# Moving ScalarE's log/exp table request and one small DVE copy in a two-layer trunk step

## The reference, cut to what matters

```python
sh1, sc1, g1, sh2, sc2, g2 = split(silu(c) @ ada_w[l] + ada_b[l], 6)
h = rms_norm(x, norm1_g[l]) * (1.0 + sc1) + sh1
x = x + g1 * mixer(h)
h = rms_norm(x, norm2_g[l]) * (1.0 + sc2) + sh2
x = x + g2 * ((silu(h @ w1) * (h @ w3)) @ w2)        # d_ff = 2816
# after both layers: y = rms_norm(x, final_norm_g)
```

## Time and profile before

| | |
|---|---|
| median of 3 runs (lowest, highest) | 1216.4 us (1214.42, 1217.55) |
| the profiled execution: time, span | 1215.29 us, 1213.5 us |
| PE busy | 1115.3 us, 92% |
| ACT busy, DVE busy, POOL busy | 399.1, 432.7, 544.4 us |
| PE's share of the chain that ended last | 72% |
| mean granted TensorE clock | 0.951 of full speed |

### The profile page before, as it was taken

How to read it: one execution, slowest core, us unless ns; L and a number is a source line. 1 busy time by engine, 2 the same in 40 slices (tenths; PEclk the granted TensorE clock), 3 DMA queues, 4 the chain that set the end, 5 groups by cost and what they waited for, 6 DMA issues and landing times.

```text
span 1213.5 us, 17339 instructions
## 1 busy us (share of the span) xinstructions
PE 1115.3 (92%) x7181; PEld 1028.0 (85%) x7181; DVE 432.7 (36%) x860; ACT 399.1 (33%) x617; POOL 544.4 (45%) x422
## 2 busy tenths in 40 slices
PE   5699998999798999999999799879998999999997
PEld 3598997896697999999999698655597999999997
DVE  4616899217665111111111230537565111111121
ACT  0532421244325322232222232447515333323221
POOL 0355576360053555455455533221053556565662
PEclk9799998899798999999999899879998999999998
DMA  9633422639525766664566821142025544434441
GB/s 311 192 105 105 140 70 70 199 132 313 157 71 139 219 196 175 184 195 142 174 211 189 219 82 42 31 101 70 2 70 139 140 110 133 129 104 129 125 123 52
DMA packets 243017, 166.46 MB, mean 137 GB/s; under 512 B 20269, under 2 KB 241532, under 8 KB 242812
## 3 DMA queue, kind: packets, MB, share of 16 engines
q1 hardware_dynamic: 214880, 135.74, 38.8%
q10 hardware_dynamic: 28060, 29.63, 7.6%
HBM read 162.43 MB, written 2.92 MB: 136 GB/s over the span
## 4 chain that ended last, share of the span: by engine, by line
PE 72%; DVE 13%; DMA 5%; POOL 4%; ACT 3%; issue 2%; ACTq 0%; SPq 0%; DVEq 0%
PE banks L431 19%; PE banks L432 18%; PE banks L433 18%; POOL w_lo L1040 4%; PE banks L505 3%; DMA raw<-in_ada_w 3%; DVE ht L1513 2%; PE banks L471 2%; ACT w_hi L1064 2%; PE banks L472 2%; PE banks L473 1%; DVE h_lo L1504 1%; DVE Kd L1697 1%; DVE Qd L1697 1%; PE banks L518 1%
## 5 line engine op out<-in xcount | busy, mean ns | idle before, releaser
L1040 POOL TENSOR_TENSOR w_lo<-raw,w_hi 128x512 fp32r<-128x512 f32 (+2 forms) x410 | 537.7, 1342 | 637.3 <-ACT w_hi L1064 637.3
L431 PE MATMUL banks<-h_hi,w_hi 128*128 128x384 f32 x1088 | 373.3, 343 | 20.8 <-DVE h_lo L1504 11.5
L432 PE MATMUL banks<-h_lo,w_hi 128*128 128x384 f32 x1088 | 368.4, 339 | 0.0
L433 PE MATMUL banks<-h_hi,w_lo 128*128 128x384 f32 x1088 | 368.1, 338 | 0.0
L1064 ACT ACTIVATE w_hi<-raw 128x2048 fp32r<-128x2048 f32 (+4 forms) x115 | 193.5, 1683 | 259.8 <-PE banks L433 169.2
L431 PEld LDWEIGHTS banks<-h_hi,w_hi 128*128 128x128 f32 x1088 | 207.3, 191 | 32.8 <-issue 29.2
L432 PEld LDWEIGHTS banks<-h_lo,w_hi 128*128 128x128 f32 x1088 | 207.3, 191 | 0.6
L433 PEld LDWEIGHTS banks<-h_hi,w_lo 128*128 128x128 f32 x1088 | 207.1, 190 | 0.6
L1567 DVE TENSOR_TENSOR uf<-sa,banks 128x384 f32<-128x384 f32 x44 | 24.4, 554 | 330.2 <-PE banks L433 324.2
L431 PE MATMUL banks<-u_hi,w_hi 128*128 128x384 f32 x352 | 119.8, 340 | 1.0 <-POOL w_lo L1040 1.0
L433 PE MATMUL banks<-u_hi,w_lo 128*128 128x384 f32 x352 | 118.3, 336 | 0.0
(11 more groups left out here) (308 smaller groups left out, 1175.8 us busy)
## 6 DMA issues: line engine op xcount, KB each, us to landing
raw<-in_ffn_w SPq DMA_DIRECT2D x88, 512.0 KB, 5.2
raw<-in_ada_w SPq DMA_DIRECT2D x28, 1024.0 KB, 7.1
raw<-in_ffn_w SPq DMA_DIRECT2D x32, 704.0 KB, 4.6
vada_raw<-in_ada_w ACTq DMA_DIRECT2D x20, 1024.0 KB, 6.6
raw<-in_w_in_even SPq DMA_DIRECT2D x18, 1024.0 KB, 5.3
raw<-in_w_out_even SPq DMA_DIRECT2D x4, 1024.0 KB, 5.9
raw<-in_w_in_odd SPq DMA_DIRECT2D x3, 1024.0 KB, 7.0
raw<-in_w_in_odd SPq DMA_DIRECT2D x8, 256.0 KB, 4.2
```

Source lines behind the costliest of these rows:

```text
L431: pe.matmul(out, s_hi, m_hi, start=first and j == 0, stop=False)
L432: pe.matmul(out, s_hi, m_lo, start=False, stop=False)
L433: mm = pe.matmul(out, s_lo, m_hi, start=False, stop=last and j == len(terms) - 1)
L1040: ins = pool.tensor_tensor(w_lo[s % SPLIT][:, at:to], raw[u % RAW][:, at:to], w_hi[s % SPLIT][:, at:to].bitcast(F32), ALU.subtract)
```

## The change

The request for the log/exp set leaves `norm` and stands once ahead of norm 0; a new request stands in `ffn` behind the loop over the 22 blocks, and the one ahead of the final norm goes. In DVE's `norm` the modulation step is done at tile 1, behind `low(0)`, where it was at tile 0 ahead of `low(0)`. Each of these places has one pair, so `modulation(place)` is the same work.

```diff
@@ ACT: def norm(n, base)
-                act.preload_act_table_set("natural_log_exp_and_others")
                 bk = misc.filled(act, ("stat", n))
@@ ACT: def ffn(l, n), loop over f
                     act.activation(u_hi[:, f, :], uf[:, f % 2, :], ACT.Copy).then_inc(S["uhi_ready"], 1)
+                act.preload_act_table_set("natural_log_exp_and_others")
                 if l == 1:
@@ DVE: def norm(n, base, place), loop over m
                     if m:
                         low(m - 1)
-                    if place is not None:
-                        modulation(place, ada_pairs(place)[m:m + 1])
+                    if place is not None and m == 1:
+                        modulation(place)
```

## The result

The changed kernel takes 1219.28 us (median of 6 runs, 1216.45 to 1221.42) where the kernel before took 1214.91 in the 6 runs beside it (1208.49 to 1217.55): a ratio of 1.0044, 95% interval 1.0024 to 1.0064. By the medians it is slower by 4.4 us; the interval goes from 2.9 to 7.8 us. The profiled execution took 1219.62 us, with a span of 1217.8.

What follows compares the result with a forecast made beforehand. PE, busy 92% of the span, was taken as the bound. Terms -0.41 - 1.44 - 0.41 + 1.35 + 1.37 = +0.46, plus 1.7 for one clock fall, gave +2.2 on 1216.4: 1218.6 us, range 1213.7 to 1220.8.

Steps and rivals of the forecast that it cites:

- The request in the FFN: Load behind each FFN's last u_hi delays the second down unit's split: 1.35 and 1.37 us slower, all on the path.
- The clock: Half clock behind PE's two lengthened down-projection waits: 45% each, one fall booked at +1.7 us, bounds 0 and 3.4.
- The row that the odds leaned on: PE's wait of 1.74 us at 792.74, followed by 3.4 us at half clock, 1.7 us of work lost.
- Two falls: Rival: clock falls at the second unit of both down projections, 1.7 us each; +3.9 in all, 1220.3 us; chance 0.16.
- The load in norms 1 and 3: Without its load Ln starts 0.79 us earlier; with the row moved, 0.41 us gained at each of norms 1 and 3.
- Norm 2: One ht and one low part go ahead of DVE's wait for PE's ada product: 1.44 us gained, bounds 0.8 and 2.2.
- Norm 0 and the final norm: Norm 0 keeps the same load at the same place; the final norm's was followed by idle ACT: 0 for both.
- A request is never skipped: Reading of the profile: the norms' request gives four real loads of 1283 ns, even where the set is loaded already.
- A drain at each load: Rival: a drain of about 1.38 us beside each new FFN load adds 2.8 us; +3.2, 1219.6 us; chance 0.02.
- hidden FFN loads: Rival: something else holds POOL's or ACT's start behind the FFN loads, only gains stay: -2.3, 1214.1 us; chance 0.06.
- the full gains of the heads: Rival: PE, not DVE's last low part, paces the first products; norms 1 to 3 give 5.4: -2.7, 1213.7 us; chance 0.06.
- the change is void: Rival: compiler puts its own load ahead of the norms' Ln, only the move gains: near 1217 us; chance 0.02.

Runs made afterwards that it cites:

- e2: Changed kernel with the FFN request one instruction earlier, directly behind the last Silu and ahead of the last u_hi: 1210.97 us, ratio 0.9982 to the kernel before.
- e5: Kernel before with only the two FFN requests added behind the last u_hi: 1220.04 us, ratio 1.0045.
- e1: The changed kernel again, unaltered: 1216.82 us, ratio 1.0027 to the kernel before.
- e3: Changed kernel with the DVE edit undone, so only the table requests change: 1216.29 us, ratio 1.0018 to the kernel before.
- e6: Changed kernel with each FFN request written twice for the same set: 1218.92 us, ratio 1.0037 to the kernel before.
- e4: Changed kernel with all ACT edits undone, so only the ada row moves: 1213.55 us, ratio 0.9995 to the kernel before.
- e7: The e2 kernel with 0.8 us of unread ACT copies added behind the last u_hi: 1212.86 us, ratio 0.9995 to the kernel before.
- e8: The e2 kernel with the ada row copied behind the norm's last low part: 1210.84 us, ratio 0.9973 to the kernel before.
- e10: The e2 kernel with the ada row back ahead of the low part of tile 0: 1212.50 us, ratio 0.9987 to the kernel before.
- e11: Same kernel as e8, timed on the chip of e10: 1210.03 us, ratio 0.9961 to the kernel before.
- e9: Changed kernel with a request for another set (exp_and_others) ahead of each FFN request: 1219.16 us, ratio 1.0031 to the kernel before.

## Why the prediction came out as it did

The forecast was 1218.6 us, slower than before by 2.2 and within the 3.6 us that a measurement was said to tell. It came out slower by 4.4, beyond that, a case given 0.15; the time, 1219.28 us, lies in the range. The mechanism was right. One term, the clock, was booked too small for the profiled execution.

- *The request in the FFN*: forecast 1.35 and 1.37 us on the path; the waits of PE grew by 1.32 and 1.36. Shown by e2 (it goes when the request moves by one instruction) and e5 (it comes with the requests alone).
- *The clock*: I gave each wait 45% and booked one fall, 1.7 us. The profiled execution had both, 1.57 and 1.59 us. Over the profiled executions of five kernels with waits of 1.77 to 1.88 us (changed, e1, e3, e5, e6) the clock fell behind 7 of 10. That is more than the 45% booked, though 7 or more of 10 would come about once in ten times at 45%. With 7 of 10 the expected loss is 0.60 + 1.4 x 1.58 = 2.8 us (an estimate from these rows), within e1's interval of 1.3 to 5.2 and just below that of the first comparison, so part of the 4.4 may be chance. It fell behind none of the 14 waits up to 1.29 us in the other seven profiles at these two places (before, e2, e4, e7, e8, e10, e11).
- *The row that the odds leaned on*: one wait of 1.74 us in layer 1, at 792.74. The wait is in all thirteen profiles, 1.74 us each time, and half clock followed within 1.4 us in ten of them, and not in e4, e7 and e9. One row could not tell such odds. The first row here is from e5, the second from e4:

```profile
798.58:801.98 3.40, 3.40 (x20) 3.40 (x19) 0.00 (x0) 1.19 (x2) 0.00 (x0) 0.54 1.09 252
793.07:796.47 3.40, 3.40 (x31) 3.40 (x30) 0.00 (x0) 1.47 (x3) 0.00 (x0) 1.00 1.03 259
```

- *Two falls*: the two-fall rival, which I gave 0.16, describes the profiled execution: it booked +3.9; the norms, the waits and the two falls sum to 3.8, and chance elsewhere brings the span to 4.3 us longer. The page of the Trainium skill cited for it, "TensorE: Matmul & The Clock Gate", section "HAM oscillation — how this bites in real kernels", names what the profiled execution did (granted clock 0.53 and 0.52 behind the two waits). But its case is a kernel whose work on each tile is shorter than the wait for the next, and here e3, e5 and e9 show waits of 1.77 to 3.03 us with full clock behind them; as a rule for every wait of this kind it does not hold in these runs.
- *The load in norms 1 and 3*: Ln forecast 0.79 us earlier, measured 0.80. The last low part forecast 0.41 us earlier, measured 0.36 and 0.32. The pieces at the head came as forecast too. What the forecast didn't ask is what the row would do at its old place once Ln is earlier: e3 shows that the table edit alone moves the last low part 1.02 us forward, and the move takes 0.66 of it back. The rows of the kernel before could not tell it, since the row's copy ran behind POOL's end there. So the forecast 0.41 was right for the change, but it missed that in these two norms one half of the change undoes most of what the other half gives.
- *Norm 2*: forecast 1.44 us, measured 1.43, by the mechanism named: the row is copied 12.26 us behind the split, before 12.23, and one `ht` pair and one low part more stand ahead of it. But the same code gave 2.53 in e2 and 1.26 in e1. In e2 PE began the ada product 9.89 us behind the split and took 1.07 us for it, and DVE did not wait; in e1 it began at 10.44 and took 1.93. The exact hit is partly luck.
- *Norm 0 and the final norm*: forecast 0; the loads are as forecast, one at norm 0 and none at the final norm.
- *A request is never skipped*: true of the norms' requests in the kernel before, not of two side by side (e6).
- *A drain at each load*: the next ACT instruction starts 1.30 us behind the start of the load here too (582.30 to 583.60), and the load starts 0.02 us behind the end of `u_hi`., which the forecast used against the drain, is a load of a set that was in place already; this one is a real switch, from Silu's set, and so is the load ahead of the first Silu in the kernel before, with 1.29 us from its start to the Silu's (383.62 to 384.91). So these rows, and not the earlier trace rows, decide against the drain that the page "ScalarE: Activation LUTs" of the Trainium skill, section "What ACT_TABLE_LOAD costs", puts beside a switch.

So the rivals with hidden FFN loads (1214.1) and with the full gains of the heads (1213.7) are refuted by the waits and by the table, and the one in which the change is void by the trace: no load stands in norms 1 to 3. The sum without clock, +0.46, stands against +0.60 from the measured terms.

## What to carry to other kernels

Before moving a fixed cost to an "idle" place, name the next instruction on that engine and who waits for it: one instruction earlier the same load was free, one later it cost 1.35 us at each of two places and often half the clock for 3.4 us behind it. When a small operation is moved off the head of a chain, look at what takes its slot: an operation that another engine blocks may end up where an unblocked one was running for nothing. And where single executions differ by more than the effect, compare distances inside the traces first. Price a fall of the clock from how often it followed over several traces, not from one row.

## What the runs showed of the hardware that was not expected

- The `ht` operations of DVE, on two SBUF inputs, are held while POOL subtracts in SBUF (128x128: 1.35 us in place of 0.35); a DVE copy out of PSUM at the same moment is not (0.68 us at 369.54 in e3, and 0.68 at 372.93 in the changed kernel, with POOL idle).
- A wait of PE of 1.8 or even 3.03 us does not always bring the low clock: in e3 twice and in e5 and e9 once each it stayed full, at the two places where it fell in other profiles.
- The wait of 1.74 us in layer 1, the same in all thirteen profiles, had half clock behind it in ten and full clock in three.
- Two adjacent requests for one table set give one load (e6); requests for two different sets side by side (e9) give two, 1.28 us each, back to back.
